# Seven block products instead of eight in half of the FFN's gate and up pairs

## The reference

```python
SEQ, D_MODEL, FFN_HIDDEN = 256, 2048, 5632
# h: the normed residual stream x, 256 x 2048
x = x + (silu(h @ w_gate) * (h @ w_up)) @ w_down
return rms_norm_2(x, g_final)
```

## Time and profile before

| | us |
|---|---|
| median of 3 runs | 2502.28 (2502.01 to 2502.35) |
| span of the profiled execution | 2499.9 |
| TensorE busy | 2489.9 |
| Vector busy | 1581.0 |
| Scalar busy | 1215.0 |
| GpSimd busy | 192.0 |

### The profile page before, as it was taken

The page is one execution under the profiler, slowest core; times in us unless marked ns, Lnnn a source line. Parts: engine busy times, 40 slices in busy tenths (PEclk is TensorE's granted clock), DMA queues, the critical chain, the costliest instruction groups (busy, mean ns, idle before and its releaser), DMA issues.

```text
span 2499.9 us, 29283 instructions
## 1 busy us (share of the span) xinstructions
PE 2489.9 (100%) x11070; PEld 2058.0 (82%) x11070; DVE 1581.0 (63%) x1974; ACT 1215.0 (49%) x1530; POOL 192.0 (8%) x319
## 2 busy tenths in 40 slices
PE   9999999999999999999999999999999999999998
PEld 7888788888888888888888889888888888888887
DVE  6665665665665666675767766686655555565556
ACT  6454444444555453444545556465544444444444
POOL 0010000000010100000001100010100000000000
PEclk9999999999999999999999999999999999999999
DMA  9676666666688877877678855675766666666664
GB/s 336 202 231 211 217 205 205 218 208 201 218 243 238 249 229 221 233 230 212 217 249 256 243 159 163 219 240 181 245 219 202 209 202 217 208 211 208 212 208 145
DMA packets 262428, 544.91 MB, mean 218 GB/s; under 512 B 13616, under 2 KB 19888, under 8 KB 261936
## 3 DMA queue, kind: packets, MB, share of 16 engines
q1 hardware_dynamic: 241152, 477.38, 59.2%
q0 software_dynamic: 21168, 66.08, 9.5%
HBM read 508.29 MB, written 35.13 MB: 217 GB/s over the span
## 4 chain that ended last, share of the span: by engine, by line
PE 99%; DVE 1%; ACT 0%; issue 0%; ACTq 0%; DVEq 0%
PE job L2043 32%; PE job L2044 31%; PE job L2049 31%; PE group L2067 1%; PE att L2316 0%; PE att L2088 0%; PE group L2338 0%; PE att L2213 0%; PE att L2317 0%; PE att L2101 0%; PE att L2102 0%; PE att L2098 0%; PE att L2198 0%; PE job L2450 0%; PE att L2081 0%; PE job L2451 0%
## 5 line engine op out<-in xcount | busy, mean ns | idle before, releaser
L1191 DVE TENSOR_TENSOR lo<-raw,hi 128x1024 fp32r<-128x1024 f32 (+1 forms) x880 | 1055.5, 1216 | 680.1 <-ACT hi L685 659.8
L685 ACT ACTIVATE hi<-raw 128x1024 fp32r<-128x1024 f32 (+1 forms) x880 | 922.1, 1055 | 1110.0 <-PE job L2049 1102.7
L2043 PE MATMUL job<-hi,xh 128*128 128x512 f32 (+1 forms) x2272 | 886.9, 391 | 0.3 <-ACT hi L685 0.3
L2044 PE MATMUL job<-hi,xl 128*128 128x512 f32 (+1 forms) x2272 | 881.2, 388 | 0.0
L2049 PE MATMUL job<-lo,xh 128*128 128x512 f32 (+1 forms) x2272 | 604.9, 388 | 0.0
L2043 PEld LDWEIGHTS job<-hi,xh 128*128 128x128 f32 x2272 | 426.7, 188 | 90.9 <-issue 2.3
L2044 PEld LDWEIGHTS job<-hi,xl 128*128 128x128 f32 x2272 | 426.5, 188 | 88.9 <-issue 2.1
L2049 PEld LDWEIGHTS job<-lo,xh 128*128 128x128 f32 x2272 | 425.4, 188 | 87.6
L2043 PE MATMUL job<-hi,ah 128*128 128x512 f32 x832 | 325.8, 392 | 0.0
L2044 PE MATMUL job<-hi,al 128*128 128x512 f32 x832 | 323.8, 389 | 0.0
L2049 PE MATMUL job<-lo,ah 128*128 128x512 f32 x832 | 222.5, 389 | 0.0
(11 more groups left out here) (328 smaller groups left out, 1218.1 us busy)
## 6 DMA issues: line engine op xcount, KB each, us to landing
raw<-in_ret_w_in SPq DMA_DIRECT2D x94, 1024.0 KB, 5.2
raw<-in_pool_w_in SPq DMA_DIRECT2D x64, 1024.0 KB, 6.2
raw<-in_w_gate SPq DMA_DIRECT2D x44, 1024.0 KB, 5.3
raw<-in_w_up SPq DMA_DIRECT2D x44, 1024.0 KB, 5.2
raw<-in_w_down SPq DMA_DIRECT2D x44, 1024.0 KB, 5.0
raw<-in_ret_w_out SPq DMA_DIRECT2D x32, 1024.0 KB, 5.1
raw<-in_pool_w_out SPq DMA_DIRECT2D x32, 1024.0 KB, 5.4
raw<-in_w_in SPq DMA_DIRECT2D x28, 1024.0 KB, 6.7
```

Of the source, the lines that this page charges most:

```text
L685: act.activation(hi[:, (U.at * 2 + h) % HS, :, 0:n], src, ACT.Copy).then_inc(hi_ready, 1)
L1191: dve.tensor_tensor(lo[:, (U.at * 2 + h) % LS, :, 0:n], src, hi[:, (U.at * 2 + h) % HS, :, 0:n].bitcast(F32), ALU.subtract).then_inc(lo_re ...
L2043: pe.matmul(o, oh[:, kt, ts], w, start=first and k == 0, stop=False)
L2044: pe.matmul(o, ol[:, kt, ts], w, start=False, stop=False)
```

## The change

Gate and up of a slice become one job set. For turns 1 to 10 a unit now holds a pair v (0 to 7) of 128-row slices (slices 2v and 2v + 1), the first half of it from `w_gate`, the second from `w_up`, loaded by two transfers of 512 KB. For one pair the work is a 2 x 2 by 2 x 2 block product: token tiles by slices, times slices by (gate, up), eight block products. Pairs 0, 2, 4 and 6 (`BILINEAR`) go through seven products of sums of blocks. The sums of token blocks are made once, in and just behind turn 0 (`tokens_made`, `tokens_low` on Vector, `tokens_high` on Scalar), and kept in `sh` and `sl`. The sums of weight blocks are made for each bilinear pair on Vector (`wsums`), rounded on Scalar (`wsh`) and subtracted on Vector (`wsl`). The odd pairs stay at eight products (`plain_unit`), with the difference of the two token tiles for one of them.

The products add up in seven banks: `BANK1`, `BANK6` and `BANK7` are three of the four banks of `pair`, the others are the banks for turning and attention. At the end of the eight pairs Vector rebuilds gate and up from them (`partial_sums`, `gate_sums`), Scalar applies silu from SBUF, and `hidden` works from SBUF. The four down jobs use `pair` as before. Job numbers go on by 4 in a turn instead of 6. On all engines the loops `Fori(2, FC)` are written out as Python loops.

```diff
+KV = KT // 2
+BILINEAR = (0, 2, 4, 6)
...
+        BANK1, BANK6, BANK7 = pair[E][1], pair[1 - E][0], pair[1 - E][1]
+        BANK2, BANK4, BANK5, BANK3 = gbank[0], gbank[1], abank[0], abank[1]
...
 # sync
+            def load_pair(U, i, v):
+
+                if U.at >= RAW:
+                    sp.wait_ge(lo_ready, U.value(2, -2 * RAW + 2))
+                slot = raw[:, U % RAW]
+                sp.dma_start(slot[:, 0], rows(w_gate[0], 2 * P * v, i * NB, k=2)).then_inc(raw_landed[U % RAW], 16)
+                sp.dma_start(slot[:, 1], rows(w_up[0], 2 * P * v, i * NB, k=2)).then_inc(up_landed[U % RAW], 16)
...
 # scalar
+            drain(Pos(FJ), Pos(FU + 7), lambda t: sg[:, t, :], RS, ACT.Silu)
+
+            def ffn_turn(i):
+                U, J, I = ffn_at(i)
+                for v in range(KV):
+                    pair_high(U + v, i, v, 0)
+                    if v - 1 in BILINEAR:
+                        high_sums(i, v - 1, 1)
+                    pair_high(U + v, i, v, 1)
+                    if v in BILINEAR:
+                        high_sums(i, v, 0)
+                    if i == 1 and v < 2:
+                        tokens_high(6 + v)
+                    if v == 6:
                         hidden_high(I, ah)
...
+                act.activation(p1s[:, :], BANK1[:, :], ACT.Copy).then_inc(first_copied, 1)
+                split_hi(U + 1)
+                if i < FC - 1:
+                    split_hi(U + 2)
+                act.wait_ge(gate_made, i)
+                for t in range(TT):
+                    ins = act.activation(sg[:, t, :], sg[:, t, :], ACT.Silu, scale=RS[:, t:t + 1])
+                ins.then_inc(gate_ready, 1)
...
 # vector
+            def tokens_made(v):
...
+                then(dve.tensor_tensor(x_full, xh[:, ks, :].bitcast(F32), xl[:, ks, :].bitcast(F32), ALU.add))
+                if v in BILINEAR:
+                    dve.tensor_tensor(x_sums[:, 0], first[:, 0], second[:, 0], ALU.subtract)
+                    then(dve.tensor_tensor(x_sums[:, 1], second[:, 0], second[:, 1], ALU.subtract))
+                    then(dve.tensor_tensor(x_sums[:, 2], x_sums[:, 1], first[:, 0], ALU.subtract))
+                    dve.tensor_tensor(x_sums[:, 3], x_sums[:, 2], first[:, 1], ALU.add).then_inc(tok_made, 1)
+                else:
+                    dve.tensor_tensor(x_sums[:, 0:2], first, second, ALU.subtract).then_inc(tok_made, 1)
...
+                if n >= 6:
+                    tokens_low(n - 6)
+                if n >= 5:
+                    tokens_made(n - 5)
...
+            def bilinear_low(U, i, v):
+
+                n, w = sums_at(i, v), four(U)
+                dve.wait_ge(raw_landed[U % RAW], (U // RAW).value(16, 16))
+                dve.wait_ge(up_landed[U % RAW], up_count(i, v))
+                dve.tensor_tensor(wsums[:, 0:2, :], w[:, 0:4:3, :], w[:, 2, :].unsqueeze(1).broadcast_to([P, 2, NB]),
+                                  ALU.add).then_inc(sums13_made, 1)
+                low_of(U, 0, slice(0, 2))
+                dve.wait_ge(sums13_made, n + 1)
+                dve.tensor_tensor(wsums[:, 2, :], wsums[:, 0, :], w[:, 3, :], ALU.add).then_inc(sum2_made, 1)
+                low_sums(i, v, 0)
+                dve.wait_ge(sum2_made, n + 1)
+                dve.tensor_tensor(wsums[:, 3, :], wsums[:, 2, :], w[:, 1, :], ALU.add).then_inc(sum4_made, 1)
+                low_of(U, 1, slice(1, 2))
...
+            def ffn_turn(i):
+                U, J, I = ffn_at(i)
+                for v in range(KV):
+                    if v in BILINEAR:
+                        bilinear_low(U + v, i, v)
                     else:
+                        low_of(U + v, 0, slice(0, 2))
+                        if v - 1 in BILINEAR:
+                            low_sums(i, v - 1, 1)
+                        low_of(U + v, 1, slice(0, 2))
+                    if v == 0 and i > 1:
                         accumulate(J - 1, U, 3)
+                    if v == 1:
+                        if i == 1:
+                            first_hidden()
+                        else:
+                            hidden(i - 1)
+                    if i == 1 and v < 2:
+                        tokens_low(6 + v)
+                        if v == 0:
+                            tokens_made(7)
+                    if v == 6:
                         hidden_low(I, al, ah)
+                U = U + KV
+                split_lo(U)
+                partial_sums(i)
+                split_lo(U + 1, halves=(0,))
+                gate_sums(i, U)
+                split_lo(U + 1, halves=(1,))
+                if i == FC - 1:
+                    hidden(i)
+                accumulate(J, U + 1, 0)
+                split_lo(U + 2)
+                accumulate(J + 1, U + 2, 1)
+                split_lo(U + 3)
+                accumulate(J + 2, U + 3, 2)
...
 # tensor
+            def bilinear_unit(U, J, i, v):
...
+                wait_pair(U, 0)
+                if first:
+                    wait_drained(pe, J - (1 if i == 1 else 2))
+                    wait_drained(pe, J - (2 if i == 1 else 1))
+                ins = product(BANK1[:, :], xh[:, k, one], xl[:, k, one], hi[:, a, 0], lo[:, a, 0], first, last)
...
+                product(BANK2[:, :], xh[:, k + 1, one], xl[:, k + 1, one], hi[:, a, 1], lo[:, a, 1], opens, closes).then_inc(half_used, 1)
+                wait_pair(U, 1)
+                product(BANK3[:, :], sh[:, s, 3], sl[:, s, 3], hi[:, b, 1], lo[:, b, 1], opens, closes).then_inc(half_used, 1)
+                pe.wait_ge(sums_low, 2 * n + 1)
+                product(BANK5[:, :], sh[:, s, 1], sl[:, s, 1], wsh[:, 0], wsl[:, 0], opens, closes)
+                product(BANK7[:, :], sh[:, s, 0], sl[:, s, 0], wsh[:, 1], wsl[:, 1], first, last).then_inc(sums_used, 1)
+                pe.wait_ge(sums_low, 2 * n + 2)
+                ins = product(BANK6[:, :], sh[:, s, 2], sl[:, s, 2], wsh[:, 2], wsl[:, 2], first, last)
...
+                product(BANK4[:, :], xh[:, k + 1, two], xl[:, k + 1, two], wsh[:, 3], wsl[:, 3], opens, closes).then_inc(sums_used, 1)
```

More of the change, by code:

```diff
@@ L1110, in _ @@
                     x_across(3, n // 2 - 2, gain2, G_FFN)
+                if n >= 6:
+                    tokens_high(n - 6)
             root(RS, MS, 10)
@@ L1119, in hidden_high @@
                                rows_of(fT[:, :, :]), ACT.Copy).then_inc(t_high, 1)
[L1121 to L1137, removed]
-                        hidden_high(I, ah)
[L1139 to L1142, removed]
@@ L1148, in kept_hi @@
+            for i in range(1, FC):
+                ffn_turn(i)
             def kept_hi(n):
@@ L1966, in kept_lo @@
+            wait_drained(dve, Pos(FJ))
+            for i in range(1, FC):
+                ffn_turn(i)
             def kept_lo(n):
@@ L2432, in _, with product @@
-            ffn_turn(0, 0)
-            ffn_turn(1, 1)
-            with pe.Fori(2, FC) as i:
-                ffn_turn(i, 2)
+            for u in range(4):
+                got = (Pos(OUT4_G), group_done) if u == 0 else (Pos(X_PARTS[3] + 2 * u), xt_low)
+                unit(Pos(FU + 2 * u), Pos(FJ), xh, xl, 4 * u, start=u == 0, stop=u == 3, groups=got[0], filled=got[1])
+                unit(Pos(FU + 2 * u + 1), Pos(FJ + 1), xh, xl, 4 * u, start=u == 0, stop=u == 3)
+            def product(o, oh, ol, wh, wl, start, stop):
+                pe.matmul(o, oh, wh, start=start, stop=False)
+                pe.matmul(o, ol, wh, start=False, stop=False)
+                return pe.matmul(o, oh, wl, start=False, stop=stop)
@@ new lines, in ffn_turn @@
+            def ffn_turn(i):
+                U, J, I = ffn_at(i)
+                if i == 1:
+                    pe.wait_ge(att_read, XA + 4)
+                    pe.wait_ge(group_done, OUT4_G + 2)
+                else:
+                    pe.wait_ge(up_made, i - 1)
+                for v in range(KV):
+                    if i == 1:
+                        pe.wait_ge(tok_low, v + 1)
+                    if v in BILINEAR:
+                        bilinear_unit(U + v, J, i, v)
+                    else:
+                        plain_unit(U + v, v)
+                U = U + KV
+                pe.wait_ge(t_low, I.value())
+                pe.wait_ge(first_copied, i)
+                for j in range(4):
+                    if j == 1:
+                        pe.wait_ge(seventh_read, i)
+                    unit(U + j, J + j, ah, al, 0, start=True, stop=True)
```

263 lines of the change are left out of this document (170 added, 93 removed).

## The result

| | before | after |
|---|---|---|
| median of 4 runs, us | 2502.28 | 2522.01 (2521.77 to 2522.99) |
| span of the profiled execution, us | 2499.9 | 2520.2 |

What follows compares the result with a forecast made beforehand. TensorE's matmuls were taken to bound the kernel. The terms -27.2 + 23.6 + 9.7 + 2.0 + 0.5 = +8.6 us on a span of 2499.9, with 2.4 us outside it, gave 2511 us, range 2503 to 2522.

Steps and rivals of the forecast that it cites:

- The saving: TensorE in turns 1 to 10: 120 matmuls fewer at 0.2267 us, 27.2 us less, nothing for the products' own pace.
- a changed pace: Sign that the forecast is wrong: the pace of the matmuls on TensorE, 0.2267 us each, changes.
- The pause at a turn's start: TensorE waits for the last down job's `accumulate`, late in Vector's queue: 2.62 us at nine starts (turns 2 to 10), 23.6 us.
- the bare stall: TensorE's wait at a turn's start if Vector is not late for the fourth `accumulate`: 1.66 us.
- Turn 1: At its start TensorE waits for `first_hidden`, behind other work in Vector's queue: 9.7 us, between 8.5 and 10.5.
- The clock and the restart behind the pause: After turn 1's long wait TensorE restarts at half clock: up to 2.6 us, taken as 2.0.
- The clock at the turns: Rival: the clock falls at every turn's start, nine restarts of 2 us, 2529 us; chance 0.09.
- The 60 that the last paragraph of the forecast names: Sign: Vector's busy time in a turn should rise from 37.5 to near 60 us, overlaps counted.
- The tight spot: Third pair of a turn: sums ready at 13.5 us, wanted at 13.7; taken as zero, upper bound 0.5 us a turn.
- The rival *same: Vector is not late at a turn's start, stall the bare 1.66 us: 8.6 us less, 2502 us; chance 0.14.
- The end: In turn 10 `hidden` stands behind Vector's sums, so the drain for the second final unit moves: 0.5 us, bounds 0 and 1.5.
- The rival *faster: Vector's queue order costs little, turn 1's stall nears 4 us without a clock fall: 2495 us; chance 0.08.

Runs made afterwards that it cites:

- Vector's order changed: The changed kernel with the fourth `accumulate` ahead of the last two operations of the first bilinear pair in Vector's queue: 2515.6 us.
- the 32 bytes: The changed kernel with 32 unused bytes ahead of the last stage's tiles: 2523.0 us.
- turn 1's other order: The changed kernel with Vector computing turn 1's first hidden slice right behind the first bilinear pair, the last token sums behind it: 2517.5 us.
- the still tile: The changed kernel with the twelve matmuls on weight sums streaming part of the low tokens instead, result not the reference's: 2517.1 us in one run.
- the 96 bytes: The changed kernel with 96 unused bytes ahead of the last stage's tiles, so the weight sums start at a multiple of 128 bytes: 2515.1 us.
- the layout turned round: The changed kernel with `raw`, `hi`, `lo` and `X` allocated behind the last stage's tiles in SBUF: 2594.7 us in one run.
- the two versions that shorten the pause by one and by two and a half us: The changed kernel with the fourth `accumulate` earlier in Vector's queue, 2515.6 us; and with TensorE's wait for the last down job before its fifth product, 2510.4 us.
- the fastest version: The changed kernel with bilinear pairs 2, 4 and 6 only and 96 unused bytes ahead of the last stage's tiles: 2483.3 us.

## Why the prediction was right or wrong

**Direction, right; size, wrong by 11.7 us of span**: 20.3 us were measured where 8.6 were forecast, and the median of 2522.01 us lies at the very end of the range, a hundredth beyond it. Two terms that stood at zero make up 10.5 of the 11.7: the falls of the clock at the turns (6.4), and the slower pace of the matmuls (4.1). The others missed by 0.2 to 0.5 each.

**The saving** was taken as 27.2 us with nothing against it. The count was right (120). The sentence that failed is the one that gave the products' own pace nothing, since the final half units run one bank in a row at full pace. That row answered another question: the bank was the same there, but the streamed tile (`hi_kept`, `lo_kept`) was one of the aligned ones. The changed operation's new operands, `wsh` and `wsl`, had no row before, and no bound was set for them. It cost 4.1 us; with it the saving is 23.1. The closing paragraph of the forecast did name a changed pace as a sign that it is wrong.

**The pause at a turn's start**: 2.62 us forecast, 2.60 and a slow second matmul of 0.08 measured. That makes 2.68 against 2.62. Both of its parts were tried: with Vector's order changed the bare stall is 1.63 and 0.08 (1.66 forecast). This is the part that a timeline gives to less than a tenth, because every row of it was there in another place.

**Turn 1**: 9.7 us forecast, 9.92 measured. Scalar's drain ended at 1815.7 instead of 1815.2, and the chain behind it took 11.7 us, what its rows say. TensorE's turn 0 ended 0.4 us later too. The clock and the restart behind the pause: 2.0 forecast, 1.6 measured. The windows of the pause and of the time behind it, in the changed kernel:

```profile
1820.00:1822.00 2.00, 0.00 (x0) 0.00 (x0) 2.00 (x4) 1.46 (x2) 0.00 (x0) 0.67 0.00 0
...
1827.00:1831.00 4.00, 3.25 (x8) 2.61 (x9) 3.25 (x5) 0.25 (x1) 0.72 (x1) 0.51 0.91 309
```

The granted clock went down at 1820.7 (the mean of 0.67), 2.7 us after the end of TensorE's last matmul at 1817.99, and was at half until 1830.9 (the mean of 0.51), 3.2 us after the restart at 1827.75.

**The clock at the turns**: this is the term that was mis-sized most, and the first step that failed. It stood among the rivals as all or nothing, nine falls at 18 us with 0.09, and at zero in the sum. Measured: four falls of nine, 6.4 us. So a pause of 2.6 us is a matter of how often, and not of yes or no. With half of the nine at 2 us, a count that no row of before could give, the sum would have been 2520. That the same pause brings the clock down only at times is shown, in one profiled execution of each kernel: behind pauses of 2.60 us four of nine here, with the 32 bytes and with turn 1's other order, three with the still tile, two with the 96 bytes. The length of the pause doesn't rank them: with the layout turned round the pauses are 2.42 us, shorter, and the clock fell behind seven of nine. What decides it stays open.

**Vector** doesn't bind inside a turn, as forecast: TensorE waits nowhere else in turns 1 to 10, and the third pair's sums arrive in time: in turn 8 they are ready at 2306.97 and wanted at 2307.43. The window of turn 7, which answers to the earlier trace rows, has Vector (the third of the busy times) at 56.6 us of 65, as its sum of 56.5 says:

```profile
2227.00:2292.00 65.00, 63.20 (x276) 51.75 (x276) 56.61 (x64) 33.02 (x37) 3.04 (x5) 1.00 0.66 210
```

The 60 that the last paragraph of the forecast names was too high: the overlaps it counted on are not in the windows. The tight spot was real as well: the two versions that shorten the pause by one and by two and a half us run into the third pair at once, with 0.68 and 0.75 us. But the margin at the sums was 0.46 us and not 0.2, and the piece that TensorE then waits for is the low half of up, a few matmuls ahead of the sums that the forecast named. The rival *same* needed a Vector that isn't late; it was.

**The smaller terms**: the extra token work made TensorE wait once in turn 0 (0.34 us, where I had it hidden), 0.4 us. The end cost 0.9 instead of 0.5.

**The rival that was right in kind** is the one on the clock, with a rate below one. The rival *faster* was wrong for this kernel, and what the forecast set against it, that both stalls are given by order and not by load, is what the fastest version uses.

## What to carry to other kernels

Work that is cut from the bound engine is only saved where the next engine's queue lets it through: the same algebra with three pairs instead of four, the first of them two places later, where no bank is still being drained, turned +19.7 us into -15.4. Read a new wait with everything that stands ahead of its releaser in that engine's queue, and price a pause of TensorE of a few us with a share of clock falls, not with none or all. Give a tile that TensorE streams from a start at a multiple of 128 bytes; small tiles ahead of it are enough to spoil it (here `posi`, of two elements, is the last of them).

## What the runs showed of the hardware that was not expected

- The pace of a fp32r matmul of 512 columns at full clock is 0.2267 us when the streamed tile starts at a multiple of 128 bytes in its partition, and 0.2333 to 0.235, as a mean over twelve, when it starts 32 or 64 bytes beyond one. Moving `hi` and `lo` off alignment cost the whole kernel 73 us (one run; some 5 of them are three more falls of the clock).
- The granted clock fell to half behind some pauses of 2.60 us and not behind others of the same length, and behind seven of nine of 2.42 us; each fall lasted 3.41 us and cost 1.60 behind the pauses of 2.60. Behind pauses of 1.63 us (nine, one kernel) and of 1.20 (nine, one kernel) none was seen. Matmuls whose result nobody reads, run in the pause, kept the clock up and made the kernel 5.5 us faster.
- The first matmul behind a wait, at full clock, has its successor 0.31 to 0.34 us behind it, not 0.23.
